# One stage of a decoder step: 40 fp32 projections become sums of three products of rounded parts

## The chip, the cores and the metric

The kernel is one program on one core of a Trainium2 chip. TensorE (PE) multiplies matrices, VectorE (DVE), ScalarE (ACT) and GpSimd (POOL) do the element-wise work, SyncE (SP) issues transfers. ACT and POOL can issue transfers too. The metric is the time of one execution on the device in microseconds (us), lower is better.

## The reference

The reference is one inference step of a decoder layer for 512 prompt tokens and 32 sample tokens (8 sequences of 4), T = 544 tokens in all, with a model width of 1024. One combined projection feeds three branches:

```python
cq, ckv_raw, kr_raw, z, xbc, dt_raw, mq, g_raw = _split_in(x_prompt @ w_in)
...
o_ssm, ssm_p = _mamba(z, xbc_ext, dt_raw, s0, *ssm_w)      # 4 groups of 8 heads
...
m  = sig(gA)*(oA@WoA) + sig(gB)*(oB@WoB) + sig(gM)*(oM@WoM);  x1 = LN(alpha*x + m@w_out)
y  = LN(alpha*x1 + relu(x1@w_up+b_up)^2 @ w_down + b_down)
```

All tensors are float32. The part that matters here is `x @ w_in` for z and xBC (and for cq, ckv and kr, which come at the end of the stage): 40 column blocks of 128 of the projection, each a 1024-deep product over all 544 tokens.

## The kernel before, in words

x lies transposed in SBUF as 8 chunks of 128 rows by 544 tokens (`X`, tensor `xt`). The weights are a stream of blocks of 128 x 1024 fp32 (512 KB), each the 8 chunks of one 128-column block. SP loads them one after another into a ring of 4 slots (`load`, L574); slot use is counted by the semaphore `blocks_begun`, which PE raises with the first matmul of every block.

`project` (L1825) multiplies one block: two halves of 272 tokens, 8 fp32 matmuls each, into one of two PSUM accumulators, `acc[0]` or `acc[1]`. The trace records an fp32 matmul as two instructions, so a projection is 32 of them. The stages after the SSM use another form (`three_products`, L1842): weights and x are each a rounded part in the type fp32r ("high") and the rest ("low"), and the product is high x high + high x low + low x high, 48 matmuls of fp32r, each one instruction. There ACT rounds a block (L749) and DVE subtracts (L1549).

The SSM stage is four groups of 10 projections. In group g the projections are called here p0 to p9. p0 to p3 make z of this group; p4 to p9 make xBC of the next group (in the last group cq, ckv and kr). Between them stand the state-space products of group g. The order of every engine is written out by hand, and each engine works strictly in that order. The names used below:

- ACT: `z_read` (reads z from acc), `evac` (L780, copies acc to the convolution's input), `decays(h)` for heads 0 to 7 (L854 x4, L857, L858), `silu`, `square`.
- DVE: `conv` and `finish` (the convolution of the next group), `weigh(h)` (L1401, decay times C.B), `add_state(b)` for 8 sequences (L1462), `gate_y`.
- POOL: `scale_c(h)` (L494), the decay of the 8 sample states (L500, b = 0 to 7, with `scale_c(4)` and `scale_c(5)` between b = 3 and b = 4).
- PE: `read_out(hp)` (L2075, L2081) for head pairs 0 to 3, which waits for `weigh` and `scale_c` of its two heads; `state_adds(b)` (L2116), which waits until DVE has done `add_state` two sequences earlier.

On PE the end of a group runs: p3, read_out(0), p4, read_out(1), p5, p6 (state_adds(0) in its middle), read_out(2), state_adds(2), p7 (state_adds(4) in its middle), read_out(3), p8 (state_adds(6)), p9. On ACT: z_read of p3, decays(2), decays(3), evac of p4, decays(4), decays(5), silu, decays(6), evac of p5, decays(7), silu, two squares, evac of p6, and so on. On DVE `weigh(7)` stands before `add_state(0)` and `add_state(1)`, then the convolution of p6 and a `finish` stand before `add_state(2)` and `add_state(3)`.

## Time and profile before

| | |
|---|---|
| median of 3 runs | 1672.19 us (1671.03 to 1673.26) |
| the profiled execution, its own time | 1671.78 us |
| its span, first to last instruction | 1669.7 us |
| granted TensorE clock, mean | 0.991 |
| PE busy | 1623.7 us (97%) |
| DVE, ACT, POOL busy | 781.7, 453.3, 407.7 us |

The SSM stage runs from about 62 to 453 us of the span. "Busy" is time in which at least one instruction ran. Every time in a timeline is counted from the start of the span. A timeline row gives its start, its length, the engine, the line of the kernel, the operation, output and inputs, and how many instructions were merged in it; a bracket says how long the engine had been idle before and which instruction ended that.

### The profile page before, as it was taken

The page shows a single profiled execution, that of the slowest core. Times are in us where ns is not written, and L with a number is a line of the kernel's source. Part 1 is how long each engine was busy: PE and PEld are TensorE (multiplying, and loading weights), DVE is VectorE, ACT ScalarE, POOL GpSimd, SP SyncE. Part 2 cuts the span into 40 slices and gives each one's busy share as a digit, 9 for nine tenths or more (in the row PEclk, how much of TensorE's full clock was granted, in tenths as well). Part 3 has the DMA queues.
Part 4 walks back from the last instruction along what each step waited for, and adds up shares of the span by engine and source line. Part 5 has one row for each costly group of instructions (what it writes and reads, how often), then busy time and mean ns, then how long its engine had stood idle before and what let it go on. Part 6 is the DMA issues. An engine that isn't in the chain of part 4 may idle for free.

```text
span 1669.7 us, 27037 instructions
## 1 busy us (share of the span) xinstructions
PE 1623.7 (97%) x10950; PEld 1408.9 (84%) x10950; DVE 781.7 (47%) x1350; ACT 453.3 (27%) x857; POOL 407.7 (24%) x344
## 2 busy tenths in 40 slices
PE   8999999999999999999999999999988999999995
PEld 6878787787878888888888877789988999999995
DVE  5657676765343222223333223253488751077234
ACT  2252433425332222222122111142234111111122
POOL 0041231403120000001244200124444334444432
PEclk9999999999999999999999999999999999999998
DMA  5424234252362222224788766422322323222221
GB/s 182 160 78 165 95 114 140 84 184 82 101 231 64 76 76 76 64 76 149 255 273 272 247 246 246 174 89 89 93 72 64 89 89 88 86 84 86 88 64 54
DMA packets 71853, 210.62 MB, mean 126 GB/s; under 512 B 10321, under 2 KB 26962, under 8 KB 66866
## 3 DMA queue, kind: packets, MB, share of 16 engines
q1 hardware_dynamic: 51824, 155.99, 29.5%
q10 hardware_dynamic: 13762, 31.93, 5.4%
q0 software_dynamic: 6144, 20.98, 3.5%
q8 instruction: 86, 1.41, 0.3%
q14 instruction: 37, 0.30, 0.1%
HBM read 194.01 MB, written 14.86 MB: 125 GB/s over the span
## 4 chain that ended last, share of the span: by engine, by line
PE 84%; DVE 7%; ACTq 3%; ACT 2%; issue 2%; DMA 1%; SPq 0%; POOL 0%; DVEq 0%
PE acc L1902 30%; PE acc L1835 21%; PE acc L1848 9%; PE acc L2208 4%; PE acc L2171 3%; PE acc L2154 2%; ACTq L1014 1%; ACTq L1012 1%; PE bank L2222 1%; PE bank L2241 1%; PE bank L2223 1%; DVE work L1303 1%; PE bank L2294 1%; PE bank L2326 1%; PE bank L2189 1%
## 5 line engine op out<-in xcount | busy, mean ns | idle before, releaser
L1835 PE MATMUL acc<-xt,ring 128*128 128x272 f32 x1504 | 358.9, 395 | 0.0
L1835 PEld LDWEIGHTS acc<-xt,ring 128*128 128x128 f32 x1504 | 282.4, 190 | 67.7 <-issue 12.0
L1902 PE MATMUL acc<-x_parts,f_parts 128*128 128x272 f32 x1408 | 219.6, 291 | 10.7 <-DVE x_parts L1230 6.2
L544 POOL TENSOR_TENSOR f_parts<-ring,f_parts 128x1024 fp32r<-128x1024 f32 x65 | 158.5, 2439 | 247.2 <-ACT f_parts L764 247.0
L1902 PEld LDWEIGHTS acc<-x_parts,f_parts 128*128 128x128 f32 x1408 | 196.0, 191 | 13.4 <-issue 6.0
L1902 PE MATMUL acc<-f_parts 128*128 128x272 f32 x1344 | 172.3, 289 | 0.0
L522 POOL DMA_DIRECT2D work<-in_page_cols x128 | 69.0, 539 | 422.2 <-PE bank L2262 382.0
L1902 PEld LDWEIGHTS acc<-f_parts 128*128 128x128 f32 x1344 | 170.4, 188 | 0.1
L1848 PE MATMUL acc<-work_high,high 128*128 128x272 f32 x464 | 138.4, 298 | 0.0
L764 ACT ACTIVATE f_parts<-ring 128x1024 fp32r<-128x1024 f32 x65 | 68.8, 1059 | 239.2 <-PE acc L1902 204.5
L1848 PE MATMUL acc<-work_high,ring_low 128*128 128x272 f32 x464 | 133.8, 288 | 0.0
L1848 PE MATMUL acc<-x_low,high 128*128 128x272 f32 x384 | 110.7, 288 | 0.0
L1848 PEld LDWEIGHTS acc<-work_high,high 128*128 128x128 f32 x464 | 87.2, 188 | 5.7 <-issue 5.3
L1848 PEld LDWEIGHTS acc<-work_high,ring_low 128*128 128x128 f32 x464 | 87.7, 189 | 0.0
L1549 DVE TENSOR_TENSOR ring_low<-ring,high 128x1024 fp32r<-128x1024 f32 x32 | 39.2, 1224 | 86.7 <-ACT high L749 86.4
L1798 DVE TENSOR_SCALAR f_parts<-attended 128x544 fp32r<-128x544 f32 x32 | 76.5, 2390 | 1.1
L1848 PEld LDWEIGHTS acc<-x_low,high 128*128 128x128 f32 x384 | 73.0, 190 | 0.2 <-issue 0.2
L1303 DVE SCALAR_TENSOR_TENSOR work<-work,vecs 128x600 f32<-128x600 f32 x72 | 68.5, 951 | 2.4
L1902 PE MATMUL acc<-f_parts,mg_parts 128*128 128x272 f32 x528 | 68.8, 289 | 0.0
L544 POOL TENSOR_TENSOR mg_parts<-ring,mg_parts 128x1024 fp32r<-128x1024 f32 x21 | 51.0, 2426 | 70.8 <-ACT mg_parts L764 70.8
L1902 PEld LDWEIGHTS acc<-f_parts,mg_parts 128*128 128x128 f32 x528 | 67.3, 188 | 0.2
L1902 PE MATMUL acc<-x_parts,mg_parts 128*128 128x272 f32 x480 | 62.1, 289 | 0.6 <-DVE attended L1792 0.6
(369 smaller groups left out, 2508.7 us busy)
## 6 DMA issues: line engine op xcount, KB each, us to landing
ring<-in_stream SPq DMA_DIRECT2D x216, 512.0 KB, 3.6
work<-in_page_cols POOLq DMA_DIRECT2D x128, 160.0 KB, 5.1
attended<-in_ssm_state ACTq DMA_DIRECT2D x8, 1024.0 KB, 6.3
work<-cum_rows SPq DMA_DIRECT2D x32, 256.0 KB, 4.5
out_ssm_s<-attended ACTq DMA_DIRECT2D x8, 1024.0 KB, 5.6
work<-in_ckv_rows ACTq DMA_DIRECT2D x64, 128.0 KB, 3.6
work<-in_ckv_rows SPq DMA_DIRECT2D x64, 128.0 KB, 2.6
work<-in_memk_cols SPq DMA_DIRECT2D x8, 1024.0 KB, 7.2
```

What stands on the lines that cost most here:

```text
L522: pool.dma_start(keys[kq][:, i * KEYS_W:(i + 1) * KEYS_W], page_cols[ids[kq * 4 + i]]).then_inc(sem[f"keys_in_slot{kq}"], 16)
L544: pool.tensor_tensor(lo, ring[:, s * BLOCK:(s + 1) * BLOCK], hi.bitcast(F), SUB).then_inc(sem["split_ready"], 1)
L764: act.activation(hi, ring[:, s * BLOCK:(s + 1) * BLOCK], ACT.Copy).then_inc(sem["hi_ready"], 1)
L1303: dve.scalar_tensor_tensor(out=c, in0=ext[j][:, i:i + CL], scalar=tap(i), in1=c, op0=MUL, op1=ADD).then_inc(sem[signal], 1)
L1549: dve.tensor_tensor(ring_low[:, of], ring[:, of], W_HIGH[i % 2].bitcast(F), SUB).then_inc(sem["split_ready"], 1)
L1798: dve.tensor_scalar(hi, q, 1.0, None, MUL).then_inc(sem["dve_step"], 1)
L1835: m = pe.matmul(acc[p][:, half, 0:width], w[:, k * P:(k + 1) * P], x(kk)[:, half * width:(half + 1) * width], start=kk == 0, stop=kk == n_ ...
L1848: m = pe.matmul(out[:, half, 0:HT], w[:, k * P:(k + 1) * P], x[k][:, of], start=k == 0 and n == 0, stop=last and k == KC - 1 and n == 2)
L1902: m = pe.matmul(acc_half, w[:, k * P:(k + 1) * P], x[:, kk, of], start=kk == 0 and n == 0, stop=kk == last and n == 2)
L2154: m = pe.matmul(acc[p][:, 0, 0:N_MEM], w[:, k * P:(k + 1) * P], mem[:, k, :], start=k == 0, stop=k == KC - 1)
L2171: m = pe.matmul(acc[p][:, half, 0:HT], w[:, c * 256 + off:c * 256 + off + P], cq[:, c, half * HT:(half + 1) * HT], start=c == 0, stop=c == 2)
L2208: m = pe.matmul(acc[1][:, half, 0:HT], w[:, k * P:(k + 1) * P], BR[:, KC + k, half * HT:(half + 1) * HT], start=False, stop=k == KC - 1)
```

## The change

The 40 projections of the SSM stage use `project_parts_of_x`: 48 fp32r matmuls on parts of weights and of x in place of 16 fp32 matmuls.

- Weights. SP no longer loads these 40 blocks. POOL issues a transfer from DRAM fp32 to SBUF fp32r, which rounds on its way (`round_weights`, semaphores `w_rounded0/1`). ACT writes the negative of the rounded block to one of three buffers (`negate`). POOL then issues a second transfer of the same block that adds the fp32 values to that buffer (`rest_of_weights`, semaphore `w_rest`), so that it holds weight minus rounded weight. A new accumulating transfer is issued only when the one before has landed.
- x. ACT rounds the 8 chunks during the first convolutions and DVE subtracts; the rests take the place of x (`x_low` lies over `xt`), so DVE follows the last fp32 projection chunk by chunk (`x_read`). The parts are kept until the heads stage, where they were made before.
- Around it: some semaphores are shared, some buffers are moved, the memory tokens are loaded when the last block of the stage has begun, and a second time before the sample stage.

```diff
+            def round_weights(i):
+                at = SSM_AT + i
+                s = at % RING
+                if i < SSM_SPLIT:
+                    pool.wait_ge(sem["blocks_begun"], CREDIT["blocks_begun"] + at - RING + 2)
+                    pool.dma_start(ring_parts[:, s * BLOCK:(s + 1) * BLOCK], stream[at]).then_inc(sem[f"w_rounded{i % 2}"], 16)
+
+            def rest_of_weights(i):
+                if i < SSM_SPLIT:
+                    if i:
+                        pool.wait_ge(sem["w_rest"], 16 * i)
+                    pool.wait_ge(sem["negated"], i + 1)
+                    pool.dma_start(W_LOW[i % 3], stream[SSM_AT + i], accum_op=ADD).then_inc(sem["w_rest"], 16)
+
+            def weights_ahead(g, q):
+                i = g * (GC + QC) + q
+                round_weights(i + 3)
+                rest_of_weights(i + 2)
...
+                weights_ahead(g, 3)
                 for h in range(4):
                     scale_c(h)
+                weights_ahead(g, 4)
                 pool.wait_ge(sem["s_off_ready"], t.next("s_off_ready"))
                 for b in range(DEC_BATCH):
                     pool.tensor_tensor(by_head(st_s[:, b, :]), by_head(st_s[:, b, :]), heads(dec_s, b, g, P),
                             MUL).then_inc(sem["st_dec_ready"], 1)
                     if b == 3:
                         scale_c(4), scale_c(5)
+                weights_ahead(g, 5)
                 scale_c(6), scale_c(7)
...
+            def negate(i):
+                s = (SSM_AT + i) % RING
+                if i < SSM_SPLIT:
+                    act.wait_ge(sem[f"w_rounded{i % 2}"], 16 * (i // 2 + 1))
+                    if i >= 3:
+                        act.wait_ge(sem["blocks_begun"], CREDIT["blocks_begun"] + SSM_AT + i - 3 + 2)
+                    act.activation(W_LOW[i % 3], ring_parts[:, s * BLOCK:(s + 1) * BLOCK].bitcast(F), ACT.Copy,
+                            scale=-1.0).then_inc(sem["negated"], 1)
...
                 ahead(0)
+                negate(first + 7)
                 act.wait_ge(sem["y_ready"], t.next("y_ready"))
                 decays(4)
                 decays(5)
...
                 ahead(1)
+                negate(first + 8)
                 decays(7)
...
+            for c in range(KC):
+                if c < KC - 1:
+                    dve.wait_ge(sem["x_read"], c + 1)
+                else:
+                    dve.wait_ge(sem["acc0_ready"], 1 + QC // 2)
+                rest_of_chunks(XL, X, XH, (c,))
             conv(0, 5)
...
+            def project_parts_of_x(p, between=None):
+                pe.wait_ge(sem[f"acc{p}_free"], t.next(f"acc{p}_free"))
+                s, i = (used.next() - 1) % RING, split_in_ssm.next() - 1
+                pe.wait_ge(sem["w_rest"], 16 * (i + 1))
+                w_high, w_low = ring_parts[:, s * BLOCK:(s + 1) * BLOCK], W_LOW[i % 3]
+                three_products(acc[p], w_high, w_low, XH, XL, True, 0, None if i else "low_even")
+                if between:
+                    between()
+                m = three_products(acc[p], w_high, w_low, XH, XL, True, 1)
                 m.then_inc(sem[f"acc{p}_ready"], 1)
```

How this stands in the engines' rows. First POOL before, from the four `scale_c(0..3)` to `scale_c(6), scale_c(7)`; `work` holds the scaled C rows, `attended` the sample states:

```order
L494 TENSOR_TENSOR work<-work 128x384 [waits e_ready] x4
L500 TENSOR_TENSOR attended<-attended,work 128x512 [waits s_off_ready]
L500 TENSOR_TENSOR attended<-attended,work 128x512 x3
L494 TENSOR_TENSOR work<-work 128x384 [waits e_ready] x2
L500 TENSOR_TENSOR attended<-attended,work 128x512 x4
L494 TENSOR_TENSOR work<-work 128x384 [waits e_ready] x2
```

POOL in the changed kernel at the same place; `ring_parts` is the rounding transfer, `work_high` and `high` are the buffers of the accumulating one:

```order
L540 TENSOR_TENSOR work<-work 128x384 [waits e_ready] x4
L502 DMA ring_parts<-in_stream 128x1024 [waits blocks_begun]
L509 DMA work_high<-in_stream 128x1024 [waits negated,w_rest]
L548 TENSOR_TENSOR attended<-attended,work 128x512 [waits s_off_ready]
L548 TENSOR_TENSOR attended<-attended,work 128x512 x3
L540 TENSOR_TENSOR work<-work 128x384 [waits e_ready] x2
L548 TENSOR_TENSOR attended<-attended,work 128x512 x4
L502 DMA ring_parts<-in_stream 128x1024 [waits blocks_begun]
L509 DMA high<-in_stream 128x1024 [waits negated,w_rest]
L540 TENSOR_TENSOR work<-work 128x384 [waits e_ready] x2
```

The transfers of block p7 (rounding) and p6 (rest) now stand behind `scale_c(3)`, and those of p8 and p7 behind the decay of sequence 7.

Next ACT before, from the silu behind decays(5) to decays(7); the first L854 group is decays(6), the last is decays(7), L780 and L781 are the evac of p5:

```order
L787 ACTIVATE work<-work 128x600 [waits conv_done]
L854 ACTIVATE work<-work 128x128 [waits cum1_loaded,y_ready]
L854 ACTIVATE work<-work 128x128 x3
L857 ACTIVATE work<-work 128x512 [waits act_step]
L858 ACTIVATE work<-work 128x384
L780 ACTIVATE work<-acc 128x544 [waits acc0_ready]
L781 ACTIVATE work<-acc 128x8x4
L854 ACTIVATE work<-work 128x128 x4
L857 ACTIVATE work<-work 128x512 [waits act_step]
L858 ACTIVATE work<-work 128x384
```

ACT in the changed kernel at the same place:

```order
L847 ACTIVATE work<-work 128x600 [waits conv_done]
L923 ACTIVATE work<-work 128x128 [waits cum1_loaded,y_ready]
L923 ACTIVATE work<-work 128x128 x3
L926 ACTIVATE work<-work 128x512 [waits act_step]
L927 ACTIVATE work<-work 128x384
L840 ACTIVATE work<-acc 128x544 [waits acc0_ready]
L841 ACTIVATE work<-acc 128x8x4
L835 ACTIVATE high<-ring_parts 128x1024 [waits blocks_begun,w_rounded0]
L923 ACTIVATE work<-work 128x128 x4
L926 ACTIVATE work<-work 128x512 [waits act_step]
L927 ACTIVATE work<-work 128x384
```

One row is new, the negation of block p8 with its wait for the rounding transfer, and it stands ahead of decays(7).

## Rows read from the trace of the kernel before

**Rows 1.** The page's first part: busy time and share of each engine
```profile
PE 1623.7 (97%) x10950; PEld 1408.9 (84%) x10950; DVE 781.7 (47%) x1350; ACT 453.3 (27%) x857; POOL 407.7 (24%) x344
```
**Rows 2.** Timeline of PE: three fp32 projections, and what follows
```profile
47.48 22.27 PE L1835 MATMUL acc<-xt,ring 128*128 128x272 f32 x96
...
69.59 1.04 PE L2027 MATMUL bank<-cst,branch 128*128 128x128 f32 x8
```
**Rows 3.** Timeline of PE, heads stage: second matmul of a three-product projection, and its successor
```profile
510.52 0.29 PE L1848 MATMUL acc<-x_low,high 128*128 128x272 f32 x1
...
516.45 1.25 PE L2234 MATMUL bank<-cst,work 128*128 128x128 f32 x10
```
**Rows 4.** Timeline of PE, second SSM group: read_out(0), state_adds(2), state_adds(4), next group's read_out(0)
```profile
199.15 0.66 PE L2075 MATMUL bank<-work 128*64 128x128 f32 x8 [0.56 <-DVE work L1401]
...
231.40 0.73 PE L2116 MATMUL bank<-rounded 96*128 96x512 f32 x2
...
235.88 1.10 PE L2116 MATMUL bank<-rounded 96*128 96x512 f32 x2
...
297.42 0.66 PE L2075 MATMUL bank<-work 128*64 128x128 f32 x8 [0.56 <-DVE work L1401]
```
**Rows 5.** Timeline of ACT, same group: decays(4), silu behind decays(5), evac of p6
```profile
211.12 1.27 ACT L854 ACTIVATE work<-work 128x128 f32<-128x128 f32 x4
...
215.62 0.69 ACT L787 ACTIVATE work<-work 128x600 f32<-128x600 f32 x1
...
229.83 0.62 ACT L780 ACTIVATE work<-acc 128x544 f32<-128x544 f32 x1 [0.78 <-PE acc L1835]
```
**Rows 6.** Timeline of POOL, same group: scale_c(5), states b = 4 to 7
```profile
215.79 1.22 POOL L494 TENSOR_TENSOR work<-work 128x384 f32<-128x384 f32 x1 [1.01 <-ACT work L858]
216.97 4.50 POOL L500 TENSOR_TENSOR attended<-attended,work 128x512 f32<-128x512 f32 x4
```
**Rows 7.** Timeline of DVE, same group: weigh(6) and (7), add_state(0) and (1), add_state(2) and (3)
```profile
228.28 1.29 DVE L1401 TENSOR_TENSOR work<-work 128x512 f32<-128x512 f32 x2
229.48 1.28 DVE L1462 TENSOR_TENSOR attended<-attended,bank 128x512 f32<-128x512 f32 x2
...
235.13 1.29 DVE L1462 TENSOR_TENSOR attended<-attended,bank 128x512 f32<-128x512 f32 x2
```
**Rows 8.** Timeline of ACT, heads stage: rounding one weight block
```profile
499.87 1.05 ACT L749 ACTIVATE high<-ring 128x1024 fp32r<-128x1024 f32 x1
```
**Rows 9.** Landing of the ring's transfers (L584) issued from 69 to 440 us
```profile
DMA to landing us min/median/max: 3.5/3.7/7.3
```
**Rows 10.** Landing of the cum rows (L594), two of 256 KB at a time
```profile
DMA to landing us min/median/max: 4.1/4.5/11.6
```
**Rows 11.** POOL's own transfers (L522, 160 KB): issue in ns, then landing
```profile
L522 POOL DMA_DIRECT2D work<-in_page_cols x128: 536/538/707, 480.2 to 941.5; - x128
...
DMA to landing us min/median/max: 2.7/5.1/8.2
```
**Rows 12.** The page's sixth part: issues, KB each, median us to landing
```profile
work<-in_mem_t SPq DMA_DIRECT2D x1, 1024.0 KB, 4.9
...
out_ckv<-work ACTq DMA_DIRECT2D x1, 544.0 KB, 9.5
```
**Rows 13.** Timeline of DVE: end of finish(0,3), conv(0,5), end of finish(0,5); subtraction of x chunks
```profile
60.04 0.18 DVE L1313 SCALAR_TENSOR_TENSOR branch<-work 128x32 f32<-128x32 f32 x1
...
63.20 0.17 DVE L1291 TENSOR_SCALAR work<-work 128x3 f32<-128x3 f32 x1 [2.77 <-ACT work L781]
...
68.20 0.18 DVE L1313 SCALAR_TENSOR_TENSOR work<-work 128x32 f32<-128x32 f32 x1
...
460.62 2.62 DVE L1543 TENSOR_TENSOR x_low<-xt,work_high 128x544 fp32r<-128x544 f32 x4
```
**Rows 14.** PE behind its longest wait (timeline), and the granted clock there (windows, PEclk)
```profile
1250.29 1.70 PE L1902 MATMUL acc<-x_parts,f_parts 128*128 128x272 f32 x6 [5.60 <-DVE x_parts L1230]
...
1250.00:1255.00 5.00, 2.58 (x10) 2.29 (x11) 4.90 (x8) 2.69 (x6) 4.43 (x6) 0.50 0.00 0
```

More of the change, by code:

```diff
@@ L143 @@
 HEAD_SPLIT = len(SPLIT_AT)
+SSM_AT = blocks_before("ssm")
+SSM_SPLIT = GROUPS * (GC + QC)
 def loaded_before(block, slot):
-    return len(range(slot, block, RING))
+    return sum(not SSM_AT <= at < SSM_AT + SSM_SPLIT for at in range(slot, block, RING))
 CREDIT = {"acc0_free": 1, "acc1_free": 1, "blocks_begun": 8, "keys_used": 4,
@@ L196, in program @@
         x_low = sb("x_low", KC * T, R)
-        high = sb("high", 2 * BLOCK + T, R)
+        with ExitStack() as whole_spare:
+            spare = whole_spare.enter_context(nc.sbuf_tensor("spare", [P, 2 * BLOCK + 2 * T], F))
+        high = sb("high", 2 * BLOCK + 2 * T, R)
         mark = sb("mark", 2, F, 1)
@@ L278, in program @@
         ext, cacc, th = ([k(EXT) for _ in range(2)] for _ in range(3))
-        krope, a_rstd = k(T), k(T)
-        late_sq = [k(T) for _ in range(2)]
-        k_rstd = late_sq[0]
+        low_at = k.at
+        krope = work[:, low_at:low_at + T]
+        x_high_at = low_at + BLOCK
+        k.at = low_at + 4 * T
+        assert x_high_at + 2 * T <= k.at
         after_conv = k.at
@@ L289, in program @@
         bc = [k(2 * T).rearrange("p (c t) -> p c t", t=T) for _ in range(2)]
+        cum_at = k.at
         cum_r = [k(SEQ) for _ in range(4)]
+        a_rstd, k_rstd = (work[:, cum_at + i * T:cum_at + (i + 1) * T] for i in range(2))
         b_last = work[2 * NS:NS3, k.at:k.at + P]
@@ L312, in program @@
         xw_full = xdt[NS:2 * NS, NB, :]
-        mem = k(KC * N_MEM).rearrange("p (c m) -> p c m", m=N_MEM)
+        x_high_too_at = k.at
+        k(3 * T)
+        mem = spare[:, 0:KC * N_MEM].rearrange("p (c m) -> p c m", m=N_MEM)
+        mem_again = work[:, xdt_at:xdt_at + KC * N_MEM].rearrange("p (c m) -> p c m", m=N_MEM)
         decay = [xw[:, c, :] for c in range(NB)]
@@ L359, in program @@
         for_heads = k.at
-        a_sq = [bc[0][:, 0, :], bc[0][:, 1, :], late_sq[0], late_sq[1], work[:, b_tm_at:b_tm_at + T]]
+        a_sq = [bc[0][:, 0, :], bc[0][:, 1, :], *(work[:, late_sq_at + i * T:late_sq_at + (i + 1) * T] for i in range(2)),
+                work[:, b_tm_at:b_tm_at + T]]
+        assert late_sq_at + 2 * T <= cum_at - 4 * T
         q_n = k(T)
@@ L794, in latent @@
                 act.activation(a_sq[i], dst, ACT.Square).then_inc(sem["squares_ready"], 1)
+            for c in range(0, KC, 2):
+                act.wait_ge(sem[f"x{c // 2}_loaded"], 32)
             evac(1)
+            round_chunks(XH, X, range(2))
             evac(0)
@@ L813, in _ @@
             act.activation(dec_s, bank[0][:, 0:DEC_BATCH * SSM_HEADS].rearrange("p (b h) -> p b h", h=SSM_HEADS),
-                    ACT.Exp).then_inc(sem["dec_ready"], 1)
+                    ACT.Exp).then_inc(sem["exps_ready"], 1)
             evac(1)
+            round_chunks(XH, X, range(6, KC))
+            negate(1)
             silu(0)
@@ L862, in _ @@
                     act.dma_start(o["conv"], conv_out).then_inc(sem["stored"], 16)
+                negate(first + 2)
                 z_read(0)
+                negate(first + 3)
                 if g:
@@ L873, in _ @@
                 z_read(1)
+                negate(first + 4)
                 z_read(2)
+                negate(first + 5)
                 act.wait_ge(sem["seg_s_ready"], t.next("seg_s_ready"))
@@ L881, in _ @@
                 z_read(3)
+                negate(first + 6)
                 act.wait_ge(sem["add_ready"], t.next("add_ready"))
@@ L916, in _ @@
                 ahead(2)
+                negate(first + 9)
                 ahead_silu(2)
                 ahead(3)
+                negate(first + 10)
                 square(2)
@@ L922, in _ @@
                 ahead(4)
+                negate(first + 11)
                 square(3)
@@ L1823, in next_block, with project @@
                 return ring[:, s * BLOCK:(s + 1) * BLOCK]
-            def project(p, x, n_blocks=1, width=HT, between=None):
+            def project(p, x, n_blocks=1, width=HT, between=None, read=None):
                 pe.wait_ge(sem[f"acc{p}_free"], t.next(f"acc{p}_free"))
@@ L1839, in project @@
                                 m.then_inc(sem["blocks_begun"], 1)
+                            elif half and read and k < KC - 1:
+                                m.then_inc(sem[read], 1)
+                m.then_inc(sem[f"acc{p}_ready"], 1)
+            def project_parts_of_x(p, between=None):
[7 more added lines that the diff above has]
+                m = three_products(acc[p], w_high, w_low, XH, XL, True, 1)
                 m.then_inc(sem[f"acc{p}_ready"], 1)
@@ L2040, in _ @@
                 m.then_inc(sem["b_turned"], 1)
-                project(0, of_x, between=lambda: turn(2, 3))
+                project_parts_of_x(0, between=lambda: turn(2, 3))
                 turn(4)
@@ L2061, in _ @@
                 states(0, 1)
-                project(0, of_x, between=lambda: states(2, 3))
+                project_parts_of_x(0, between=lambda: states(2, 3))
                 def read_out(hp):
```

153 lines of the change are left out of this document (81 added, 72 removed).

## The prediction

> **What bounds the kernel now.** I read the page's first part, then the timeline of PE over the SSM stage, then ACT, POOL and DVE over one of its groups, then the transfers. PE is busy for 97% of the span [rows 1], and over the 98.3 us from one group's read_out(0) to the next (297.42 - 199.15) its only listed wait is 0.56 us [rows 4]. So time that PE no longer needs is gained at once, unless another engine is late in its place. The sum is made against the profiled execution's 1671.8 us, 0.4 below the median of 1672.2.
>
> **What the change removes.** Three fp32 projections take 69.59 - 47.48 = 22.11 us, 7.37 each [rows 2]. In a three-product projection 47 matmuls start in 516.45 - 510.52 = 5.93 us, 126 ns apart; 48 make 6.06, and I put 0.03 on it for the start of a block: 6.09 [rows 3]. The saving is 1.28 us a projection, 12.8 a group, 51.2 for all 40.
>
> **What it adds beside PE.** Per projection: a negation on ACT, 1.05 us by the rounding of a block of the same shape [rows 8], and two transfers issued by POOL at 0.54 us each [rows 11]. Per group that is 10.5 us on ACT and 10.8 on POOL. Both are free for more than half of a group, so as mere work it costs nothing; what counts is where it stands and what it waits for.
>
> The trace shows no transfer that converts or accumulates. For the rounding one, r from issue to landing, the ring's own 512 KB give 3.5 at the least and 3.7 in the median [rows 9], POOL's smaller transfers 5.1 in the median and 8.2 at most [rows 11]. I take r = 4.5, the median of the cum transfers, 512 KB in two that fly in this same stretch [rows 10]. For the accumulating one, d: it reads two sides of 512 KB, and 1 MB lands in 4.9 us [rows 12]; behind the rounding one on the same queue I take 6.5. Its lower end is the 3.5 of one plain block, its upper end the longest landing of the cum rows, 11.6 [rows 10]. Neither can be below nothing, since the data must arrive.
>
> **Wait one, at read_out(0).** It hangs on DVE, which starts its last steps with the state products in the middle of p3; the second half of p3 is now 0.64 us shorter, so PE waits 0.56 + 0.64. Loss 0.64 a group.
>
> **Wait two, at state_adds(2).** Count from the end of p3 (198.59 in this group). PE reaches state_adds(2) at 231.40 - 198.59 = 32.8 before, now at 32.8 - 3 x 1.28 + 0.64 = 29.6. The chain that it needs:
> - The negation for p6 needs its buffer free, so p4 must have begun: 1.2 wait + 1.7 read_out = 2.8, with the negation 4.0. decays(2) and (3) take 2.25 each, as decays(4) and (5) took 4.5 (215.62 - 211.12) [rows 5]: 8.5. scale_c(3) is done at 9.6, and only then POOL issues the rounding transfer of p7.
> - It lands at 9.6 + r. Negation 10.7 + r, decays(4) and (5) 15.2 + r, scale_c(5) 1.2 and the states b = 4 to 7 4.5 [rows 6]: 20.9 + r. Only then POOL issues the rounding transfer of p8.
> - It lands at 20.9 + 2r, and ACT waits for it ahead of decays(7): negation 22.0 + 2r, decays(7) usable 1.9 later, weigh(7) 0.65, add_state(0) and (1) 0.65 each [rows 7]: 25.85 + 2r, and 0.1 to PE.
>
> PE waits 25.95 + 2r - 29.6 = 2r - 3.65: 5.35 us at r = 4.5, and 3.35 at 3.5.
>
> **Wait three, at state_adds(4).** ACT ends decays(7) at 24.25 + 2r = 33.25, then silu 0.7, two squares 1.3, evac of p6 0.8: 36.05. From the end of that evac (229.83 + 0.72 = 230.55 [rows 5]) to the end of add_state(3) (236.4 [rows 7]) DVE took 5.9: 41.95. PE starts p7 at 34.95 + 0.57, is in its middle at 38.55, and could issue the second product at 38.85. It waits 3.1 us, in the three groups that have convolutions beside them. The last group has none.
>
> The accumulating transfer of p7 leaves POOL at 20.9 + 4.5 + 0.54 = 25.9 and lands at 32.4, under wait two. Those of p8, p9 and the next p0 follow each other from 35 on at d + 0.3, and PE needs one every 6.1 to 9 us behind a start at 47: hidden at d = 6.5, with 1 to 3 us to spare.
>
> **The start.** DVE ends finish(0,3) at 60.22, then subtracts 8 chunks at 0.655, 65.5, then does the 5.4 us of conv(0,5) and its two finishes: 70.9 [rows 13]. PE ends p0 at 69.59 - 1.28 = 68.3 and waits 2.6. The parts of x that are no longer made between the SSM and heads stages gain nothing, as PE did not wait for them. The memory tokens have 13 us to land and took 4.9 [rows 12]: nothing.
>
> **Sum.** -51.2 + 4 x 0.64 + 4 x 5.35 + 3 x 3.1 + 2.6 = -51.2 + 35.9 = -15.3. 1671.8 - 15.3 = 1656.5 us.
>
> **A rule to weigh.** In no row of before does POOL issue a transfer while DVE is in a dense stretch; its issues take 536 to 707 ns [rows 11]. The Trainium skill (SBUF, "Who interferes with whom") says that a transfer issued by GpSimd can be starved while its descriptors are written, because some DVE instructions lock a port that both use. With one DVE step of 0.6 us at each of the two issues in the chain that would be 1.2 us a group, and the sum 1661; by the row alone it is 0. I leave it out of the sum.
>
> **Rivals.**
> - *The placement hides everything.* If r counts only once, because POOL finds its transfers already landed, waits two and three vanish: -51.2 + 2.6 + 2.6 = -46, 1626 us. For it: DMA is half idle in this stage, and the ring lands in 3.7. Against it: POOL's order, in which the transfer of p8 stands behind the states. 15%.
> - *The clock falls in the new waits.* After PE's longest wait, 5.60 us, the granted clock was 0.50 from 1250 to 1255 (1.2 in place of 2.4 GHz) and full again near 1260: 8 us at half speed, about 4 lost [rows 14]. Wait two is 5.35. One fall a group costs 16 us: 1672, and a longer first wait makes it 1680. The Trainium skill (TensorE: Matmul & The Clock Gate, "HAM oscillation") has the same rule, that idle gaps bring the clock to half. Against: read_out and p6 are cut by shorter waits, of 0.6 us in the listed rows. 13%.
> - *The accumulating transfers are the bound, and the kernel is slower.* Each leaves only when the last has landed, so a projection cannot take less than d + 0.54. It decides above d = 9.3, where ten of them pass the 98.3 us of a group. By the 9.5 of a 544 KB store [rows 12] a group takes 100.4: 1671.8 + 4 x 2.1 + 2.6 = 1683. By 11.6 it takes 121.4: 1671.8 + 92 + 2.6 = 1767. For it: three sides of 512 KB, and the queue shares its engines with the rounding transfer. Against: 1 MB in 4.9. 17%.
> - *The rounding transfer alone is slow.* At r = 8.2 wait two is 12.75: -51.2 + 2.6 + 51 + 9.3 + 2.6 = +14.3, 1686. The zero is reached at r = 6.4. 9%.
>
> **How the numbers follow.** The forecast (r from 3.5 to 6, 1648 to 1668) has 46%. Within 0.2% (3.3 us, about what can be told from no change here) of before lie the top of the forecast, half of the clock's case and the mild ends of the last two: 12%. Faster is 45% of the forecast and the first rival, 60%; slower the rest, 28%. The range leaves 10% on each side: half of the first rival below 1637, and the accumulating rival's upper part above 1702. The forecast's own range is 1648 to 1668.
>
> **What would show it.** Right: 126 ns from matmul to matmul in all 40 projections; two PE waits a group, before state_adds(2) for DVE's add_state and inside p7, of some 5 and 3 us, none of the second kind in the last group; ACT idle ahead of the negations of p7 and p8 for a transfer; PE waiting about 2.6 us for DVE before the first turn. Wrong: PE waiting for an accumulating transfer at the start of projections (d above 9), ACT never idle for a transfer (first rival), or a granted clock below 0.99 in the SSM stage.

## The result, and the profile after

The changed kernel takes 1681.65 us (median of 5 runs, 1678.59 to 1686.88); the kernel before took 1672.56 beside it. The ratio is 1.0064, with a 95% interval of 1.004 to 1.0087: slower by 9 us, where 15 us less were predicted. The profiled execution has a span of 1679.8 us (before 1669.7), and its mean granted clock is 0.977 (before 0.991). The SSM stage holds the difference: from the first fp32r projection to the sums behind the last one it takes 463.33 - 62.67 = 400.7 us; the same stretch took 391.1 us before.

First part of the page of the changed kernel, to be set beside [rows 1]:

```profile
PE 1594.3 (95%) x11590; PEld 1430.8 (85%) x11590; DVE 807.8 (48%) x1350; ACT 493.3 (29%) x897; POOL 468.5 (28%) x424
```

PE has 29 us less work and yet ends later. What PE waited for from 15 to 520 us (engine, line, releaser: us in total, times, longest; lines with less than 0.7 us left out):

```profile
PE bank L2206 <- DVE attended L1548: 15.6, 4, 5.9
PE bank L2206 <- DVE branch L1565: 10.1, 3, 4.0
PE bank L2165 <- DVE work L1487: 7.5, 4, 2.2
PE acc L1938 <- DMA work_high<-in_stream: 3.5, 2, 2.9
PE bank L2117 <- DVE work L1388: 3.4, 3, 1.7
PE acc L1938 <- DMA high<-in_stream: 3.4, 2, 2.5
```

That is 43.5 us, against 0.56 us a group before [rows 4]. L2206 is `state_adds`, L1548 `add_state`, L1565 `read_y_s` (DVE reads the samples' products out of PSUM), L2165 `read_out(0)`. L2117 is the first turn of a group, which waits for the end of a convolution: 1.54 us at the start of the stage and 1.72 us in the second group. The two DMA rows are the accumulating transfers, for which PE waits ahead of p1 in three groups (0.87, 2.93 and 2.50 us) and once, 0.55 us, ahead of p9.

Timeline of PE in the second group, start, length, instruction, and in brackets the wait and its releaser; the L1938 rows are the first matmuls of half projections, and for the slow one the second too:

```profile
200.26 0.66 PE L2165 MATMUL bank<-work 128*64 128x128 f32 x8 [1.11 <-DVE work L1487]
...
211.93 0.39 PE L1938 MATMUL acc<-high,ring_parts 128*128 128x272 f32 x1
...
218.07 0.30 PE L2189 MATMUL bank<-cst,work 128*128 128x32 f32 x2
...
227.54 1.19 PE L2206 MATMUL bank<-rounded 96*128 96x512 f32 x2 [3.99 <-DVE branch L1565]
228.53 0.43 PE L1938 MATMUL acc<-high,ring_parts 128*128 128x272 f32 x1
228.75 0.43 PE L1938 MATMUL acc<-x_low,ring_parts 128*128 128x272 f32 x1
...
233.39 0.66 PE L2165 MATMUL bank<-work 128*64 128x128 f32 x8
```

The undisturbed projection p5 takes 218.07 - 211.93 = 6.14 us, near the 6.09 of the prediction. Behind the wait of 3.99 us the matmuls of p6 follow each other every 0.22 us in place of 0.126, and half a projection takes 233.39 - 228.53 = 4.86 us, where another takes 3.2. The granted clock there (windows: busy us of each engine, then PEclk, DMA share, GB/s):

```profile
222.00:226.00 4.00, 1.55 (x13) 1.32 (x11) 2.51 (x4) 1.38 (x4) 4.00 (x6) 0.95 0.00 0
226.00:232.00 6.00, 4.46 (x18) 4.30 (x19) 5.79 (x13) 2.98 (x7) 1.48 (x2) 0.50 0.75 165
```

PEclk is 0.50, that is 1.2 in place of 2.4 GHz. Nine half projections of the stage are slow in this way, each right behind a wait of 2.5 to 5.9 us; by the row starts they take 14.1 us more than 3.2 us each.

The balance of the stage: 40 x 1.30 saved = -52; listed waits 43.5 - 2.2 before = +41.3; slow halves +14.1; that makes +3.4, and the stage is 9.6 us longer. The rest, some 6 us, has several small parts, of which the row starts name two. The last matmul ahead of a wait is overlapped by nothing: the first half of p6 takes 3.29 us where a wait follows (120.43) and 3.13 where none does (424.04), some 2 us for all the new waits. And that half took 3.57 us before, so it saves 0.44 and not half of 1.30: 1.30 is the saving of an undisturbed projection, and over all 40 it is less.

Transfers issued from 62 to 460 us (KB each, median us to landing), and the share of 16 DMA engines that POOL's queue took:

```profile
q0 software_dynamic: 10901, 39.67, 46.2%
...
ring_parts<-in_stream POOLq DMA_DIRECT2D x37, 512.0 KB, 4.6
high<-in_stream POOLq DMA_DIRECT2D x25, 512.0 KB, 7.3
```

r is 4.6 us (4.5 was taken) and d about 7 (6.5 was taken), but with a tail: in the timeline of POOL, at the end of the second group, the rest for p1 is issued behind the sums of squares, and the next one can leave only when it has landed:

```profile
262.50 0.92 POOL L509 DMA_DIRECT2D work_high<-in_stream  x1
...
273.73 0.88 POOL L509 DMA_DIRECT2D high<-in_stream  x1 [9.75 <-DMA work_high<-in_stream]
```

Last, a row of DVE that has no counterpart before, and what POOL did meanwhile. The copy of 128x3 took 0.17 us in the median before, and 0.45 at most:

```profile
211.10 3.66 DVE L1366 TENSOR_SCALAR work<-work 128x3 f32<-128x3 f32 x1 [0.71 <-ACT work L841]
```
```profile
210.31 4.42 POOL L548 TENSOR_TENSOR attended<-attended,work 128x512 f32<-128x512 f32 x4
```

The states b = 0 to 3 began at 206.74 before and were over when this copy came at 211.28. Now they start behind two transfers, and the copy ends with POOL's row.

### The profile page after: what moved, and what is told of

The parts are those of the page before. It is cut to its first block, busy times and chain, and to the rows that moved or that the text cites. A ratio compares the mean times of both kernels' runs of the same rounds, so it can differ in the third digit from the quotient of the medians.

```text
span 1679.8 us, 28482 instructions
## 1 busy us (share of the span) xinstructions
PE 1594.3 (95%) x11590; PEld 1430.8 (85%) x11590; DVE 807.8 (48%) x1350; ACT 493.3 (29%) x897; POOL 468.5 (28%) x424
## 4 chain that ended last, share of the span: by engine, by line
PE 75%; DVE 6%; ACT 5%; DMA 5%; issue 3%; ACTq 3%; POOL 2%; SPq 0%; DVEq 0%; POOLq 0%
PE acc L1992 30%; PE acc L1938 16%; PE acc L1912 7%; PE acc L2298 3%; PE acc L2261 3%; DMA ring_parts<-in_stream 2%; DMA high<-in_stream 2%; PE acc L2244 2%; ACT work L923 1%; ACTq L1089 1%; ACTq L1087 1%; DMA work_high<-in_stream 1%; POOL attended L548 1%; PE bank L2312 1%; PE bank L2331 1%
## 5 line engine op out<-in xcount | busy, mean ns | idle before, releaser
L1938 PE MATMUL acc<-work_high,ring_parts 128*128 128x272 f32 x768 | 226.0, 294 | 0.0
L1938 PE MATMUL acc<-x_low,ring_parts 128*128 128x272 f32 x640 | 191.7, 299 | 0.0
L1938 PE MATMUL acc<-work_high,high 128*128 128x272 f32 x628 | 184.6, 294 | 0.0
L1938 PEld LDWEIGHTS acc<-work_high,ring_parts 128*128 128x128 f32 x768 | 149.5, 195 | 0.5 <-DVE x_low L1425 0.4
L1938 PEld LDWEIGHTS acc<-x_low,ring_parts 128*128 128x128 f32 x640 | 128.2, 200 | 3.0 <-issue 1.9
L1938 PEld LDWEIGHTS acc<-work_high,high 128*128 128x128 f32 x628 | 121.3, 193 | 0.0
L1938 PE MATMUL acc<-x_low,high 128*128 128x272 f32 x384 | 110.4, 287 | 0.0
L1938 PE MATMUL acc<-high,ring_parts 128*128 128x272 f32 x256 | 82.9, 324 | 6.9 <-DMA work_high<-in_stream 3.5
L1630 DVE TENSOR_TENSOR ring_parts<-ring,high 128x1024 fp32r<-128x1024 f32 x32 | 39.2, 1224 | 88.3 <-ACT high L800 88.1
L1938 PEld LDWEIGHTS acc<-x_low,high 128*128 128x128 f32 x384 | 72.6, 189 | 0.2 <-issue 0.2
```

The lines of the kernel that those rows point to most:

```text
L1630: dve.tensor_tensor(ring_parts[:, of], ring[:, of], W_HIGH[i % 2].bitcast(F), SUB).then_inc(sem["split_ready"], 1)
L1938: m = pe.matmul(out[:, half, 0:HT], w[:, k * P:(k + 1) * P], x[k][:, of], start=k == 0 and n == 0, stop=last and k == KC - 1 and n == 2)
```

## Experiments

Theory A was that the waits come from where the steps stand, and that waits halve the clock. Its rivals: the accumulating transfers set the pace (B), the clock falls for another reason (C), and, from the traces, POOL's row of state products holds DVE (D). The kernel before, timed beside each set of runs, took 1672.3 to 1672.8 us. "Ratio" is against it.

**1. The order of the steps.** Three runs on the changed kernel. e1_act alters ACT:

```diff
                 ahead(0)
-                negate(first + 7)
                 act.wait_ge(sem["y_ready"], t.next("y_ready"))
                 decays(4)
                 decays(5)
                 ahead_silu(0)
+                negate(first + 7)
...
                 ahead(1)
+                decays(7)
                 negate(first + 8)
-                decays(7)
```

> The changed kernel with ACT's order altered alone: the negation of p7 stands behind the silu that follows decays(5), that of p8 behind decays(7). POOL and DVE as in the changed kernel.
> Theory A (the new waits come from where the steps stand, and each wait over about 2.5 us halves PE's clock for some us): ACT no longer stands 2.3 + 5.6 us for the two rounding transfers ahead of decays(4) and decays(7). PE's wait in the middle of p6 (3.0 to 4.0 us, for read_y_s) and most of the wait for add_state (2.6 to 5.9 us) go; with them the falls of the clock at these places. Waits from 43.5 to about 20 us, clock loss from 22 to about 8: 1681.7 - 23 - 14 = about 1645 (1640 to 1660).
> Theory B (the accumulating transfers, one at a time, set the pace): the order of ACT changes nothing, 1677 to 1686, and the wait turns up before projections, for a transfer.
> Theory C (waits from placement, clock for another reason): 1681.7 - 23 = 1659, granted clock still near 0.977.

Measured 1670.5 us, ratio 0.9985 (0.9974 to 0.9997): 11 us better than the changed kernel, where 37 were expected. The wait for `add_state` nearly goes, but the one for `read_y_s` grows, from 10.1 to

```profile
PE bank L2206 <- DVE branch L1565: 17.9, 3, 6.6
```

The chain to it begins a projection earlier, in the convolution of p4. Its copy of 128x3 meets POOL's row of state products (207.06 to 211.5) and the `scale_c` right behind it, its taps run beside the next row, and the silu, which stands ahead of the evac of p5 on ACT, waits for them:

```profile
207.86 4.62 DVE L1366 TENSOR_SCALAR work<-work 128x3 f32<-128x3 f32 x1 [0.71 <-ACT work L841]
```
```profile
218.44 0.71 ACT L847 ACTIVATE work<-work 128x600 f32<-128x600 f32 x1 [6.13 <-DVE work L1378]
```

So the evac of p5 comes at 222.24, though PE had ended p5 at 214.82.

e2_pool alters POOL:

```diff
-                for h in range(4):
-                    scale_c(h)
+                scale_c(0), scale_c(1)
                 weights_ahead(g, 4)
+                scale_c(2), scale_c(3)
...
                     if b == 3:
+                        round_weights(i + 8)
                         scale_c(4), scale_c(5)
-                weights_ahead(g, 5)
+                        rest_of_weights(i + 7)
...
                 weights_ahead(g, 8)
+                rest_of_weights(i + 11)
...
-                weights_ahead(g, 9)
+                round_weights(i + 12)
```

> The changed kernel with POOL's order altered alone: the rounding transfer of p7 and the rest of p6 stand between scale_c(1) and scale_c(2), the rounding transfer of p8 ahead of scale_c(4), the rest of p7 behind scale_c(5), the rest for p1 of the next group ahead of the sums of squares. ACT and DVE as in the changed kernel.
> Theory A: the rounding transfers have landed when ACT comes to the negations; ACT's idle time for ring_parts falls from 65 to below 25 us. The chain to add_state shortens by up to 2 x 4.6 us, and the wait at p1 of the next group (2.9 and 2.5 us, for the rest) goes. About 1645 to 1660, a little better or worse than with ACT's order altered.
> Theory B: the accumulating transfers still follow each other one by one; 1677 to 1690.
> Theory C: about 1660, clock still near 0.977.

Measured 1668.75, ratio 0.9976 (0.9963 to 0.9989): 13 us better, where 22 to 37 were expected. The rest for p1 is no longer late, but the next one, for p2, is (2.8 to 3.3 us).

e5_all has both, and DVE's `add_state(0)` and `(1)` right behind the finish of p4, `add_state(2)` and `(3)` inside the convolution of p6:

```diff
                 ahead_finish(0)
+                add_state(0)
+                add_state(1)
...
-                add_state(0)
-                add_state(1)
-                ahead(2)
+                ahead(2, between=lambda: (add_state(2), add_state(3)))
                 ahead_finish(1)
-                add_state(2)
-                add_state(3)
```

> ACT's order and POOL's order altered as in the two kernels with one of them each, and DVE's too: add_state(0) and (1) stand right behind the finish of p4, ahead of gate_y(0) and weigh(6); add_state(2) and (3) stand inside the convolution of p6.
> Theory A: the waits in a group nearly vanish; what stays is read_out(0) (7.5 us in all), the start (1.5) and some of the rests at a group's end. Waits about 12 in place of 43.5, clock full: 1681.7 - 31 - 20 = 1631 (1626 to 1645), faster than both kernels.
> Theory B (accumulating transfers one at a time set the pace, 7.0 us and more each, up to 11.3): waits move to the start of the projections, for a transfer; 1660 to 1680.
> Theory C: 1650, clock still near 0.977.

Measured 1666.0, ratio 0.9965 (0.9951 to 0.9979). Faster than before, but 35 us short of theory A: this order does not remove the cause. 37 us of waits are left. The largest is one of up to 6.0 us for `read_y_s` in three groups, and the DVE row in front of it stands beside POOL's states from 217.37 on and the two `scale_c` behind them, which end at 223.6 without a gap:

```profile
219.07 4.58 DVE L1369 TENSOR_SCALAR work<-work 128x3 f32<-128x3 f32 x1 [2.49 <-ACT work L844]
```

**2. Unread matmuls inside the waits** (e4_fill, on the changed kernel):

```diff
+            def fill(p, n):
+                for _ in range(n):
+                    pe.matmul(acc[p][:, 1, HT:512], XH[0][:, 0:P], XH[0][:, 0:512 - HT], start=True, stop=True)
...
-                project_parts_of_x(1, between=lambda: state_adds(0))
+                project_parts_of_x(1, between=lambda: (fill(1, 18), state_adds(0)))
```

> The changed kernel with matmuls added on PE whose results nobody reads (fp32r, 128x240, columns 272 to 511 of an accumulator): 18 of them, about 2 us, ahead of state_adds(0) in every group and of state_adds(4) in the first three, 10 ahead of p1 of the groups 2 to 4, 30 ahead of state_adds(2) in the last group. Nothing else moves. They lie inside PE's waits (3.0 to 4.0, 2.6 to 4.0, 2.5 to 2.9, 5.9 us), so what PE waits for is as late as before, but PE idles under 2.5 us at a time.
> Theory A (idle PE of over about 2.5 us halves the clock): the granted clock returns to 0.99 and nearly all of the 22 us of clock loss comes back, less up to 3 us where the filler is longer than the wait left: about 1662 (1658 to 1668).
> Theory C (the clock falls for another reason, such as the load of the fp32r matmuls or of DMA): the filler makes it no better, 1680 to 1690, clock still near 0.977.

Measured 1678.6, ratio 1.0034 (1.0019 to 1.0048). The listed waits halve, so nearly the same time is idle or filled, and 3 us come back, in the right direction but far from 20; the interval overlaps that of the changed kernel, so the time alone shows little. Six slow halves stay in place of nine (6.7 us), three of them behind waits of only 1.37, 1.47 and 1.97 us. The size of 22 us had been summed from windows of the clock, which count idle time too; the row starts give 14.1.

**3. The clock by itself, in the kernel before.** e16_before_wait makes DVE late for `read_y_s`; e17_before_wait_fill also fills PE's wait:

```diff
                 def read_y_s():
+                    for _ in range(8):
+                        dve.scalar_tensor_tensor(out=cb, in0=cb, scalar=1.0, in1=cb, op0=MUL, op1=MAX)
```
```diff
-                project(1, of_x, between=lambda: state_adds(0))
+                project(1, of_x, between=lambda: (fill(1, 16), state_adds(0)))
```

> The kernel before, with eight more steps of DVE (128x512, about 0.68 us each) ahead of read_y_s in every group, so that PE must wait in the middle of p6, as it does in the changed kernel: 5.4 us less the 1.0 that read_y_s was early, 4.4, and about 0.5 us at state_adds(2). No transfer and no projection is changed.
> If idle PE brings the clock down: one fall a group, 1.5 us each as in the changed kernel (half a projection behind such a wait took 4.86 us in place of 3.2): 1672.3 + 4 x 4.9 + 4 x 1.5 = 1698 (1694 to 1702), granted clock below 1 behind each wait.
> If the clock fell for the fp32r products or the transfers: 1692, clock full.

> As the kernel before with the eight more DVE steps, and 16 matmuls (fp32, 128x128, some 0.22 us each, 3.5 us) whose results nobody reads stand on PE inside the wait in the middle of p6. What PE waits for comes as late as without them.
> If idle PE brings the clock down: it stays full and about 6 us come back, 1692 (1689 to 1695). Otherwise the time is as without them, 1698 or 1692, whichever that was.

Measured 1699.7, ratio 1.0161 (1.0144 to 1.0178), and 1695.1, ratio 1.0134 (1.0117 to 1.0151). PE of e16, at the wait in the second group, with the 16 fp32 matmuls that took 3.83 us before:

```profile
239.03 1.19 PE L2121 MATMUL bank<-rounded 96*128 96x512 f32 x2 [5.42 <-DVE branch L1484]
240.02 5.33 PE L1840 MATMUL acc<-xt,ring 128*128 128x272 f32 x16
```

There is no fp32r product and no POOL transfer here, so idle PE is enough for the clock to fall: 18.8 us of waits cost 27 us of time. Of the 8 us between, 4.6 come back with the filler, which still leaves waits of 1.8 us and a clock below 1 in two groups. The other way round, e20_all2_unch_fill in run 6 has the fp32r products and all the transfers, and a full clock. C is not needed. The Trainium skill (TensorE: Matmul & The Clock Gate, "HAM oscillation") has it this way too, that idle gaps of PE bring the clock to half; it speaks of longer gaps than some that were followed by slow halves here (1.4 to 2.0 us in e4_fill), and there the trace decides.

**4. POOL's unbroken row.** e10_stt writes the copies and the first tap of the convolution in another form, on the changed kernel; e12_all_stt does the same on e5_all; e11_all_gaps is e5_all with a gap between POOL's state products:

```diff
-                dve.tensor_scalar(conv_out[:, ch, 0:3], ext[j][:, SEQ:EXT_P], 1.0, None, MUL)
+                dve.scalar_tensor_tensor(out=conv_out[:, ch, 0:3], in0=a, scalar=1.0, in1=a, op0=MUL, op1=MAX)
```
```diff
                     pool.tensor_tensor(by_head(st_s[:, b, :]), by_head(st_s[:, b, :]), heads(dec_s, b, g, P),
                             MUL).then_inc(sem["st_dec_ready"], 1)
+                    pool.wait_ge(sem["st_dec_ready"], t.next("st_dec_ready"))
```

> The changed kernel, with the four TENSOR_SCALAR instructions of the convolution (three small copies and the first tap) written as SCALAR_TENSOR_TENSOR with the same values. Theory D, formed from the traces: a TENSOR_SCALAR of DVE that meets POOL's row of four state products does not start until the row is over. In the changed kernel the copy of 128x3, 0.17 us else, took 3.66 and 1.8 us in each of three groups (211.10 and 234.62), because the transfers ahead of the states moved them onto the end of evac of p4 and p6; before the change the same copies never took over 0.2 us.
> Theory D: no such step is over 0.5 us. The chain of ACT is what is late for p5, so only the second one of a group is won for PE: 1.8 us in three groups, and some clock: 1681.7 - 5 - 3 = 1674 (1668 to 1679).
> Theory A without D (the length of such a step is an artefact or harmless): 1681 +- 3.

> ACT's, POOL's and DVE's order altered (the kernel that measured 1666.0), and the convolution's TENSOR_SCALAR instructions as SCALAR_TENSOR_TENSOR. In that kernel the copy of p5 (219.07, 4.58 us) held read_y_s and so state_adds(0), PE's longest wait (16.5 us in three groups, 6.0 at most).
> Theory D: this wait falls by 4.4 us a group to about 1.5 us; waits from 38 to about 25 us, and the clock stays full in these places (12 us lost in that kernel): 1666 - 13 - 8 = 1645 (1638 to 1653).
> Without D: 1666 +- 3.

> ACT's, POOL's and DVE's order altered (the kernel that measured 1666.0), and POOL waits for its own state product before it starts the next, which leaves a gap of some 0.1 us between two. DVE as in that kernel, TENSOR_SCALAR kept.
> Theory D in the form 'the step waits for a gap in POOL's row': the 4.58 us fall to about 1.1 us, and the kernel gains nearly as much as with other instructions, 1666 - 10 - 6 = 1650 (1643 to 1658).
> Theory D' (the step is kept waiting by POOL's whole stretch whatever its gaps): 1666 +- 3.

Measured 1684.6, ratio 1.0076 (1.0058 to 1.0095); 1667.75, ratio 0.9967 (0.9957 to 0.9977); 1663.3, ratio 0.9944 (0.9927 to 0.9961). The form of the instruction is not it. In e10 the copy, merged in its row with the next one, took 3.7 us as before in each of three groups, and in e12 the two still take, beside the same row of POOL,

```profile
222.90 4.67 DVE L1366 SCALAR_TENSOR_TENSOR work<-work 128x3 f32<-128x3 f32 x2 [2.49 <-ACT work L844]
```

while with gaps the longest of all 24 copies is 1.27 us (count, shortest/median/longest in ns):

```profile
L1370 DVE TENSOR_SCALAR work<-work x24: 149/170/1269, 31.5 to 355.4; 128x3 f32<-128x3 f32 x24
```

The wait for `read_y_s` falls from 16.5 to 10.9 us. The time falls by only 2.7 us against e5_all, where 16 were expected, and the two intervals overlap: the hold is shown by the rows, its price not yet. The Trainium skill (SBUF, "Who interferes with whom") says that DVE and GpSimd share a pair of ports, and that the one which issues first can keep it for its whole instruction while the other blocks. Here the copy was held for all or most of what was left of an unbroken row of four to six instructions, and a run of steps already under way only went slower (in e1_act three taps took 4.60 us beside a row, 3.25 else); which port did it, no run shows.

**5. The accumulating transfers.** e6_norest leaves them out (so the third product is made with minus the rounded weight); e7_unchained lets two be under way at a time:

```diff
-                    if i:
-                        pool.wait_ge(sem["w_rest"], 16 * i)
+                    if i >= 2:
+                        pool.wait_ge(sem["keys_in_slot0" if i % 2 else "w_rest"], 16 * (i // 2))
```

> The changed kernel without its accumulating transfers: POOL still waits for each negation, but issues no rest_of_weights, and PE waits for the negation alone. The third product so uses minus the rounded weight, which is not what is to be computed; the work on PE, ACT and DVE is the same. 21 MB of transfers and 40 issues of 0.9 us on POOL go.
> Theory B (the accumulating transfers, one at a time, set the pace): the time falls to what the placement leaves, 1650 or below.
> Theory A (placement; the transfers only count at p1 of the groups 3 and 4 and through POOL's 0.9 us an issue): PE's waits for transfers go (6.9 us), the rounding transfers may land a little earlier (4.6 to 4.0 us, two in the chain of a group); 1681.7 - 7 - 4 = 1671 (1666 to 1676).
> Theory D (below) says the same as A here, since POOL's states stand where they stood.

> The changed kernel, in which two accumulating transfers may be under way at a time (two semaphores by turns); every order as in the changed kernel.
> If the chain costs by itself: the waits for transfers (6.9 us, at p1 of two groups) go, and POOL no longer stands up to 9.8 us for a landing, with a fall of the clock in two groups: 1681.7 - 7 - 3 = 1672 (1668 to 1675).
> If it only counts where the other waits are mended: 1679 to 1683.

Measured 1653.6, ratio 0.9882 (0.9865 to 0.9898), and 1681.5, ratio 1.0049 (1.0031 to 1.0067). Without these transfers 28 us go, where theory A allowed 11: they cost more than PE's rows name. With them out the wait at `read_out(0)` also halves (7.5 to 3.5 us), the rounding transfers land in 4.0 in place of 4.6, and five halves are slow in place of nine. Of the 28 us, 15 are listed waits (43.5 to 28.5) and 7 slow halves; 6 stay unexplained. The edit is not a clean one: POOL also issues less, so its row of states (201.87 to 205.9 in the second group) ends as the copy of p4 comes, and no copy takes over 0.92 us. The engines are crowded where the landings are late in the changed kernel: from 235 to 290 us their share is 0.9 to 1.05 in 7 of 11 windows of 5 us. So theory B holds in part. The chain alone, taken away in the changed kernel, is worth nothing there, since other waits come first.

**6. All of it.** e13_all2 has a second order for ACT, with POOL's and DVE's order of e5_all and the gaps; against the changed kernel:

```diff
                 ahead(0)
-                negate(first + 7)
...
                 decays(4)
                 decays(5)
+                negate(first + 7)
+                ahead(1)
                 ahead_silu(0)
...
                 decays(6)
-                ahead(1)
+                decays(7)
                 negate(first + 8)
-                decays(7)
```

e14_all2_unch adds the edit of e7. e19_all2_unch_nogaps is e14 without the gaps, e18_gaps the changed kernel with the gaps alone. e20_all2_unch_fill is e14 with unread matmuls inside three waits of each group:

```diff
+                fill(1, 9)
                 read_out(0)
...
-                project_parts_of_x(1, between=lambda: state_adds(0))
+                project_parts_of_x(1, between=lambda: (fill(1, 10), state_adds(0)))
...
+                fill(0, 8)
                 pe.wait_ge(sem["conv_ready"], t.next("conv_ready", QC))
```

> A second order for ACT: evac of p4, decays(4), decays(5), negation of p7, evac of p5, silu, decays(6), decays(7), negation of p8. POOL's and DVE's order as in the kernel that measured 1666.0, and POOL waits for each of its own state products before the next (the kernel with this and the first order measured 1663.3).
> There evac of p5 ended 4 us behind the end of p5, because the silu of p4, a negation and decays(6) stood ahead of it, and PE waited 3.9 us a group for read_y_s. If the place of the steps is the cause: that wait falls below 1 us, with it 1.5 us of clock loss a group: 1663 - 9 - 4 = 1650 (1645 to 1656). If the accumulating transfers bound, the waits for transfers (10 us in that kernel) grow by as much: 1660 to 1665.

> As the kernel with the second order of ACT, and two accumulating transfers may be under way at a time (two semaphores by turns; a transfer waits for the one before the last).
> If the waits for transfers come from the chain of one behind the other: they fall from 10 us to about 3, another 5 to 9 us gained, 1643 (1638 to 1650). If the DMA engines are full at the end of a group (share 0.9 to 1.05 from 235 to 290 us in the changed kernel), two at a time land later each and nothing is gained: within 3 us of the other.

> The changed kernel, in which POOL waits for each of its state products before it starts the next; every order as in the changed kernel.
> If POOL's unbroken row holds DVE: no copy of 128x3 over 1.2 us (3.66 and 1.8 us now, in three groups). The first is not what is late, the second delays add_state(2) by 1.8 us: 1681.7 - 5 = 1677 (1673 to 1680).
> Otherwise 1682, or more, as each product then costs POOL 0.1 us.

> The kernel that measured 1645.0, with POOL's state products in unbroken rows again.
> If the row holds what DVE begins in it: the copies of p5 start at about 216.5, inside the row of b = 4 to 7, and are held some 3 us, for which PE waits ahead of state_adds(0): 3 x 3 us and some clock, 1645 + 12 = 1657 (1650 to 1660).
> If the row is harmless: 1643 to 1646.

> The kernel that measured 1645.0, with 10 unread matmuls (fp32r, 128x240, about 0.11 us each) ahead of state_adds(0), 9 ahead of read_out(0) and 8 ahead of the first turn of each group: about 1 us inside each of the waits of 0.9 to 2.6 us.
> If the clock falls for what PE idles: of the seven windows with a clock below 1 (loss 9 us by the windows, about half of it in time) most go, and the filler costs up to 3 us where it is longer than the wait: 1642 to 1646, clock 0.99.
> Otherwise 1648 and clock as before.

| | us | ratio, 95% |
|---|---|---|
| e13_all2 | 1655.9 | 0.9901 (0.9885 to 0.9918) |
| e14_all2_unch | 1645.0 | 0.9831 (0.9815 to 0.9848) |
| e18_gaps | 1684.9 | 1.0079 (1.0059 to 1.01) |
| e19_all2_unch_nogaps | 1655.2 | 0.9899 (0.988 to 0.9918) |
| e20_all2_unch_fill | 1642.45 | 0.9814 (0.9797 to 0.9831) |

The same two edits, gaps and two transfers at a time, are worth nothing in the changed kernel (+3 and 0 us, with intervals that overlap that of the changed kernel) and 10 and 11 us in the mended order, clear of noise. For e18_gaps 5 us less had been expected: the first copy of a group falls from 3.7 to 0.7 us at most, as was said, but the second keeps its 1.8 us, because it lies beside a single instruction of POOL, the sum of squares of 1.7 us, in which there is no gap. The row of POOL is what the gaps mend. DVE's `weigh(4)` and `(5)`, which took 2.1 us beside POOL before, in e19 and then in e14, with POOL's row in e19 between them:

```profile
212.13 6.53 DVE L1490 TENSOR_TENSOR work<-work 128x512 f32<-128x512 f32 x2
```
```profile
212.18 4.34 POOL L549 TENSOR_TENSOR attended<-attended,work 128x512 f32<-128x512 f32 x4
```
```profile
211.95 3.46 DVE L1491 TENSOR_TENSOR work<-work 128x512 f32<-128x512 f32 x2
```

In e20 no half projection is slow, and the granted clock is full through the stage; PE's waits in it (15 to 520 us), with the clock of the whole kernel:

```profile
PE bank L2125 <- DVE work L1392: 4.1, 3, 1.8
PE bank L2214 <- DVE branch L1569: 3.8, 3, 1.4
PE bank L2173 <- DVE work L1491: 3.3, 3, 1.1
PE bank L2214 <- DVE attended L1552: 2.2, 3, 0.8
...
core 0: 1640.6 us, clock 0.993
```

It beats both kernels, by 30 us (before) and 39 us (changed). The filler is worth 2.5 us by the medians; the two intervals overlap.

## Why the prediction was wrong, step by step

- **The saving** (1.28 us a projection, 51.2 in all): right for an undisturbed projection, 1.30. Over the stage, with the waits and the slow halves taken out, PE's rows got some 46 us shorter; what is missing was in no term of the sum.
- **r = 4.5, waits two and three** (8.4 us in each of three groups, 5.35 in the last): measured 7.1, 6.6, 6.1 and 5.9. The late chain of ACT was right, and so was the second wait, inside p7 (4.0, 2.6 and 3.1 us for 3.1). The first came at another place in three groups, ahead of `state_adds(0)`, for `read_y_s`, which hangs on the same chain and which the prediction did not name; that its size is near 5.35 (3.1, 4.0 and 3.0) is in part luck. The last group's is ahead of `state_adds(2)`, as said.
- **Wait one** (1.20 us): 1.1 to 2.2, 7.5 in all in place of 4.8.
- **The start** (2.6 us): 1.54. A wait of 1.72 us at the same place in the second group was in no term.
- **d = 6.5, hidden with 1 to 3 us to spare**: failed. The median of 7.0 was near, but the engines are full at the end of a group, one landing took 11.3 us, and PE waited 6.9 us for transfers. Leaving them out was worth 28 us. "Both are free for more than half of a group" was said of ACT and POOL; of the DMA engines the sum took no account. The third rival named the right transfers, but its bound, d + 0.54 us a projection, did not set the pace at d = 7.0: with the chain taken away (e7_unchained) nothing was gained.
- **The clock**: the step that turned the sign. The sum -15.3 was built from waits of 5.35 and 3.1 us and priced each at its own length. The rival that priced the fall had 13%, on the ground that 0.6 us waits lie between. Measured: nine slow halves, 14.1 us. By the waits as they were (+41.3 us, where the sum had 35.9) and the even saving the change would still have won 11 us; with the slow halves it is +3, and with the 6 us that no term had, +9. e16 and e17 show the fall without any part of the change.
- **A cost that no step had**: moving POOL's states by two issues put them onto DVE's copies, a copy of 0.17 us that takes 3.7. Alone it cost PE nothing that the times can tell there (e18), but it is one reason why mending the order alone gave 15 us and not 50: with ACT's second order and two transfers at a time, 10 us hang on it (e19).

The first rival (the placement hides everything, 1626) did not come true even with the placement mended: 1642 is the best that was reached.

## What to carry to other kernels

Price a predicted wait of PE at its length, its unoverlapped end (0.16 us here) and the slow stretch behind it (1.6 us in the mean of nine), and do that before the sign of the sum is read. Where several causes each delay the same chain, a single edit shows nothing (0 and +3 us) that is worth 10 us once the others are mended, so test an edit in the mended kernel too. When steps are moved on an engine that shares a resource, compare what will lie beside them, and count the transfers' engine time over the busiest stretch, not over the stage.

## What the runs showed of the hardware

- Slow halves followed waits of PE of 2.5 to 5.9 us in the changed kernel. Shorter waits had them too in some cases: 1.37, 1.47 and 1.97 us in e4_fill, 1.60 in e6_norest. Others had none: three of 2.1 us in the changed kernel, and one of 3.0 us in e5_all, behind which the half took 3.1 us:

```profile
178.76 0.36 PE L1939 MATMUL acc<-high,ring_parts 128*128 128x272 f32 x1 [2.99 <-DMA work_high<-in_stream]
```

- A DVE copy of 128x3, 0.17 us else, was held for 3.7 to 4.7 us beside four to six GpSimd instructions in a row, in two instruction forms; with gaps between the state products no copy beside them took over 1.3 us (e11_all_gaps). Beside one GpSimd instruction of 1.7 us it took 1.8. `weigh` took 6.5 us for two beside the row of four.
- POOL issued a rounding transfer of 512 KB in 0.59 us and an accumulating one in 0.89 us; 75 of them, 39.7 MB, took 46.2% of the DMA engines' time over 398 us, against 23.3% for the 28.4 MB of SP's queue before.
